# Sums of weight blocks made for two tiles by one instruction, in gate and up of a SwiGLU layer

## The chip, the cores and the metric

The kernel runs on one core of a Trainium2 chip. The metric is the device time of one execution in microseconds (us), the median of several runs. Besides TensorE (PE in the profile, PEld for its weight loads) there are VectorE (DVE), ScalarE (ACT), GpSimd (POOL) and SyncE (SP), whose queue starts most transfers.

## What is computed

One layer of a hybrid decoder: a mixing part (sliding-window attention beside an RWKV-7 recurrence, merged by gates), then a SwiGLU feed-forward part, both with RMS norms and residuals, all in float32. The change lies in the feed-forward part alone:

```python
D_MODEL, SEQ, FFN_HIDDEN = 2048, 512, 5632
h = rms_norm(x, norm_ffn[l])
x = x + (jax.nn.silu(h @ ffn_gate[l]) * (h @ ffn_up[l])) @ ffn_down[l]
return rms_norm(x, norm_final)
```

## The kernel before

**Gate and up.** The two products of 512 tokens with 2048 x 5632 weights are made in 11 chunks of 512 hidden columns (`CHUNKS`, index `j`). In a chunk the weights of 2048 rows stand in two row blocks (of gate and up each), with which a scheme of Strassen's kind works: the 2 x 2 blocks 11, 12, 21 and 22 (`wblock`, each 1024 rows by 512 columns, laid out as 4 runs of 8 tiles of 128) are combined by additions, and seven products (`PRODUCTS`, made in the order 1, 7, 6, 5, 4, 3, 2) take the place of eight. The activations have their own combinations (`S_raw`, split in `S_hi` and `S_lo`), made once, the later ones in chunk 0.

**Items.** Each product has 8 items, one for each 128-row tile `k` of its weight block (`HK` is 8); a chunk has 56, the kernel 616. An item goes through three engines. ScalarE rounds the tile to a high part (`ring_high`, tile `ring_hi`, the cast of line 697). VectorE subtracts that from the tile for the low part (`ring_low`, line 1540, tile `ring_lo`). TensorE makes six matmuls from both (lines 2150 to 2154): three for each of two groups of 128 tokens. The high and low parts lie in a ring of 4 slots (`RING`), so a cast of item w waits until item w - 4 has been multiplied (`item_done`). In products 1, 3 and 2 the tile is a block as it was loaded; in 7, 6, 5 and 4 it is a combination, and the cast waits for `sums_ready` to reach `sum_of(j, product, k)`.

**The sums.** VectorE makes them in place in the blocks: `t_one` (block 11 becomes 12 - 11, used by product 5, and by `t_two`), `t_three` (block 12 becomes 22 - 12, product 7), `t_two` (block 12 becomes 22 - 11, product 6) and `t_four` (block 12 becomes 12 - 21, product 4). One instruction makes one tile of 128 rows: 128 partitions of 4 x 128 columns, 512 in all. Each counts `sums_ready` up by one. `block_wait` holds a sum until the half block (4 tiles) has been loaded.

**Order.** VectorE's queue is written out by hand, in the loops of lines 1609 to 1697: for each product of a chunk, eight times a low part and between them the sums that later products need, and the additions that join the products: `hidden1` and `hidden2` (the products of gate and up, scaled), and additions to `u2buf`, `u3buf` and `c22buf` out of PSUM. `hidden1(j - 1)` of the chunk before stands in product 1, after low parts 5 and 6. `fence()` is a drain, an instruction that lets all earlier work of VectorE finish. TensorE makes product 1, then waits for `hidden1` and turns its result by eight transposes (line 2163), then makes product 7. In chunk 0 VectorE also makes the low parts of four activation combinations (`s_late_low`, line 1588, 2048 columns each).

Of the kernel before, what the change touches and what calls it, by code (L numbers as in the profile page):

```python
# [29 lines left out]
P = 128  # L30
# [46 lines left out]
HK = KD // 2  # L77
# [51 lines left out]

def sum_of(j, product, k):  # L130

    first = {5: k + 1 + max(k - 5, 0), 7: (2 * k + 7 if k < 3 else k + 9), 6: 2 * HK + k + 1,
             4: 3 * HK + k + 1}[product]
    return j * 4 * HK + first


PARTS = ("u2", "u3", "c22", "c21", "hid2", "c12", "hid1")
# [34 lines left out]
def build_layer(nc, xT, w_slots, w_ups, w_gu, w_down, norms, pair_cst, low_mu,  # L172
# [108 lines left out]
    def place(at, name, shape, dt=f32):  # L281

        return Arena(nc, keep.at - H_BYTES - W_BYTES + at * 1024)(name, shape, dt)
# [9 lines left out]
    wblock = {b: place(block_at[b], f"wblock{b}", [CT, HK * P]) for b in block_at}  # L293
# [23 lines left out]
    with ExitStack() as ctx:  # L317
# [91 lines left out]
        def block_wait(engine, j, b, k):  # L409

            engine.wait_ge(block_loaded[b][2 * k // HK], rows_before[b] + 16 * (j + 1))
# [683 lines left out]
        def _(dve):  # L1095
# [4 lines left out]
            def fence():  # L1100

                V.drain()  # L1102
# [433 lines left out]
            def ring_low(j, product, k):  # L1536

                w = item_of(j, product, k)
                dve.wait_ge(ring_hi_ready, w + 1)
                V.tensor_tensor(ring_lo[w % RING][:], wsrc[product][:, :, k * P:(k + 1) * P],  # L1540
                                ring_hi[w % RING][:].bitcast(f32), SUB).then_inc(ring_lo_ready, 1)
# [19 lines left out]

            def of_tile(b, k):

                return wblock[b][:, :, k * P:(k + 1) * P]

            def t_one(j, k):

                block_wait(dve, j, 12, k)
                V.tensor_tensor(of_tile(11, k), of_tile(12, k), of_tile(11, k), SUB).then_inc(sums_ready, 1)
# [10 lines left out]
            def t_four(j, k):  # L1580

                block_wait(dve, j, 21, k)
                V.tensor_tensor(of_tile(12, k), of_tile(12, k), of_tile(21, k), SUB).then_inc(sums_ready, 1)
# [25 lines left out]
            for j in range(CHUNKS):  # L1609
                last = j == CHUNKS - 1  # L1610
                for k in range(HK):
                    if j or k >= 4:
                        ring_low(j, 1, k)
                    t_one(j, k)
                    if k >= 5:
                        fence()
                        t_three(j, k - 5)
                    if j and k in (5, 6):
                        hidden1(j - 1, k - 5)
                for k in range(HK):  # L1620
                    ring_low(j, 7, k)
                    if k + 3 < HK:
                        t_three(j, k + 3)
                    else:
                        fence()
                        t_two(j, k - 5)
                    if j == 0 and k == 3:
                        dve.wait_ge(ss_done, 2)
                        V.tensor_scalar(rstd, R[2][:, 0:4], 1.0 / D_MODEL, NORM_EPS, MUL, ADD
                                        ).then_inc(ms_ready, 1)  # L1630
                    if j == 0 and k == 7:
                        dve.wait_ge(rms_ready, 2)
                        V.reciprocal(rstd, rstd)
                        fence()
                        s_late_low(0, 5)
                for k in range(HK):
                    ring_low(j, 6, k)
                    if k + 3 < HK:
                        t_two(j, k + 3)
                    if j == 0 and k == 4:  # L1640
                        s_late_low(1, 4)
                    if j == 0 and k == 7:
                        s_late_low(2, 3)
                for k in range(HK):
                    ring_low(j, 5, k)
                    if k < 3:
                        fence()
                        t_four(j, k)
                    if j == 0 and k == 2:
                        s_late_low(3, 2)  # L1650
                    if k in (3, 4):
                        dve.wait_ge(item_done, after(j, 6))
                        dve.wait_ge(c_read, copied(j, "p1", k - 3))
                        V.tensor_tensor(u2buf[:, k - 3, :], u2buf[:, k - 3, :], bank_b[k - 3][:], ADD
                                        ).then_inc(c_ready, 1)
                    if k in (5, 6):
                        fence()
                        if j:
                            dve.wait_ge(hid2_stored, 16 * j)
                        else:  # L1660
                            for u in range(2):
                                dve.wait_ge(x2_stored[u], 16 * (KD // 2 + 1))
                        V.tensor_tensor(u3buf[:, k - 5, :], u2buf[:, k - 5, :], bank_of(j, 7)[k - 5][:], ADD
                                        ).then_inc(c_ready, 1)
                for k in range(HK):
                    ring_low(j, 4, k)
                    if k + 3 < HK:
                        t_four(j, k + 3)
                    if k in (3, 4):
                        dve.wait_ge(item_done, after(j, 5))  # L1670
                        if j:
                            dve.wait_ge(hid1_stored, 16 * j)
                        fence()
                        V.tensor_tensor(c22buf[:, k - 3, :], u3buf[:, k - 3, :], bank_d[k - 3][:], ADD
                                        ).then_inc(c_ready, 1)
                for k in range(HK):
                    ring_low(j, 3, k)
                    if k in (3, 4):
                        dve.wait_ge(item_done, after(j, 4))
                        fence()  # L1680
                        V.tensor_tensor(u3buf[:, k - 3, :], u3buf[:, k - 3, :], bank_b[k - 3][:], SUB
                                        ).then_inc(c_ready, 1)
                    if k == 7:
                        hidden2(j, 0)
                    if last and k >= 5:
                        g_low(0, k - 5)
                for k in range(HK):
                    ring_low(j, 2, k)
                    if k == 0:
                        hidden2(j, 1)  # L1690
                    if k in (3, 4):
                        dve.wait_ge(item_done, after(j, 3))
                        fence()
                        V.tensor_tensor(u2buf[:, k - 3, :], u2buf[:, k - 3, :], bank_d[k - 3][:], ADD
                                        ).then_inc(c_ready, 1)
                    if last:
                        g_low(0, k + 3)
# [679 lines left out]
```

## Time and profile before

| | us |
|---|---|
| median of 3 runs | 2839.48 |
| lowest and highest | 2838.54, 2843.10 |
| the profiled execution | 2841.24 |
| its span | 2839.3 |
| gate and up in it, about | 1450 to 2330 |

The page of a profile gives busy time by engine and the costliest groups of instructions. Other views are asked of the trace: the busy time of each engine in a stretch (windows), who waited for whom (waits), and the instructions in order of time (timeline). In a timeline row stand the start, the duration, engine, line, operation, written tile and read tiles, shapes and a count, and in brackets the idle time of the engine before it and who ended that. Matmuls are shown with durations that overlap; the distance of their starts is the pace. Numbers of buffers are left out of names. The bank of PSUM that a product uses is called dense or work.

### The profile page before, as it was taken

Reading aid. Unit: us, or ns where it says so; the run is one execution under the profiler, and the core shown is the slowest. Engines: PE = TensorE matmul, PEld = TensorE weight load, DVE = VectorE, ACT = ScalarE, POOL = GpSimd, SP = SyncE. Lnnn points to the kernel's source line nnn. Section 1 sums busy time; section 2 is a strip of 40 time slices with the busy share of each in tenths; the row PEclk is TensorE's granted clock in tenths of the full one; section 3 lists DMA queues with packets and bytes.
Section 4 is the critical chain, followed back from the end, with each engine's and each line's share of the span. In section 5 each row is a group of like instructions: output and inputs, shape, how many; then the busy total and the mean of one; then the engine's idle time right before and its main releaser. Section 6 shows DMA issues by size and latency. Waiting matters only on the chain.

```text
span 2839.3 us, 37234 instructions
## 1 busy us (share of the span) xinstructions
PE 2779.1 (98%) x14475; PEld 2247.7 (79%) x14475; DVE 1532.7 (54%) x2529; ACT 1120.0 (39%) x1761; POOL 794.1 (28%) x675
## 2 busy tenths in 40 slices
PE   8999999999999999999999999999999998999998
PEld 7767777777777777888877888888888876888887
DVE  5656355365365364322478888888888861111122
ACT  5444333343333343222345555555555542222222
POOL 2333333234234234545410000000000014545454
PEclk9999999999999999999999999999999999999999
DMA  5222222222222233434344443333334434333323
GB/s 185 75 75 102 81 77 94 71 78 92 74 82 92 74 115 127 155 126 155 135 154 134 126 134 108 120 107 113 122 107 134 134 118 161 133 102 133 102 92 110
DMA packets 116862, 320.08 MB, mean 113 GB/s; under 512 B 7264, under 2 KB 23904, under 8 KB 103776
## 3 DMA queue, kind: packets, MB, share of 16 engines
q1 hardware_dynamic: 108736, 303.24, 31.7%
q10 hardware_dynamic: 7968, 14.68, 1.5%
q8 instruction: 105, 1.72, 0.2%
q14 instruction: 53, 0.43, 0.0%
HBM read 285.66 MB, written 32.24 MB: 112 GB/s over the span
## 4 chain that ended last, share of the span: by engine, by line
PE 90%; DVE 4%; ACT 2%; DMA 2%; issue 1%; DVEq 1%; POOL 0%; SPq 0%; ACTq 0%; POOLq 0%
PE dense L1773 17%; PE dense L1775 16%; PE dense L1774 16%; PE work L2150 7%; PE work L2152 7%; PE work L2154 7%; PE dense L2150 2%; PE dense L2154 2%; PE dense L2152 2%; PE work L1941 1%; PE work L1993 1%; DVEq L1102 1%; PE work L1774 1%; PE work L1773 1%; PE work L1775 1%
## 5 line engine op out<-in xcount | busy, mean ns | idle before, releaser
L655 POOL TENSOR_TENSOR wlo<-raw,whi 128x512 fp32r<-128x512 f32 x400 | 540.7, 1382 | 890.6 <-ACT whi L697 890.6
L655 POOL TENSOR_TENSOR dn_lo<-dn_raw,dn_hi 128x352 fp32r<-128x352 f32 x256 | 240.5, 971 | 1137.0 <-ACT dn_hi L697 1137.0
L697 ACT ACTIVATE ring_hi<-wblock 128x512 fp32r<-128x512 f32 x616 | 388.4, 632 | 405.2 <-PE work L2154 293.0
L1773 PE MATMUL dense<-H_hi,whi 128*128 128x512 f32 x1208 | 504.9, 418 | 10.0 <-DVE H_lo L1130 8.5
L1540 DVE TENSOR_TENSOR ring_lo<-wblock,ring_hi 128x512 fp32r<-128x512 f32 x616 | 422.0, 687 | 126.5 <-ACT ring_hi L697 120.2
L1775 PE MATMUL dense<-H_hi,wlo 128*128 128x512 f32 x1208 | 473.5, 392 | 0.0
L1774 PE MATMUL dense<-H_lo,whi 128*128 128x512 f32 x1208 | 473.2, 392 | 0.0
L2150 PE MATMUL work<-ring_hi,S_hi 128*128 128x512 f32 x976 | 383.7, 393 | 14.3 <-DVE ring_lo L1540 14.3
L697 ACT ACTIVATE whi<-raw 128x2048 fp32r<-128x2048 f32 (+1 forms) x109 | 198.2, 1821 | 470.2 <-PE dense L1775 396.2
L2152 PE MATMUL work<-ring_hi,S_lo 128*128 128x512 f32 x976 | 381.4, 391 | 0.0
L2154 PE MATMUL work<-ring_lo,S_hi 128*128 128x512 f32 x976 | 381.2, 391 | 0.0
L1773 PEld LDWEIGHTS dense<-H_hi,whi 128*128 128x128 f32 x1208 | 227.6, 188 | 81.6 <-issue 27.0
L1773 PE MATMUL dense<-G_hi,dn_hi 128*128 128x512 f32 x693 | 270.7, 391 | 10.3 <-POOL dn_lo L655 10.3
L1774 PE MATMUL dense<-G_lo,dn_hi 128*128 128x512 f32 x693 | 270.2, 390 | 0.0
L1775 PE MATMUL dense<-G_hi,dn_lo 128*128 128x512 f32 x693 | 270.1, 390 | 0.0
L1775 PEld LDWEIGHTS dense<-H_hi,wlo 128*128 128x128 f32 x1208 | 227.3, 188 | 50.0
L1774 PEld LDWEIGHTS dense<-H_lo,whi 128*128 128x128 f32 x1208 | 228.0, 189 | 45.0 <-issue 5.8
L1710 DVE TENSOR_TENSOR resid<-resid,dense 128x512 f32<-128x512 f32 x63 | 43.3, 687 | 386.5 <-PE dense L1775 386.5
L697 ACT ACTIVATE dn_hi<-dn_raw 128x1408 fp32r<-128x1408 f32 x64 | 88.4, 1382 | 359.5 <-PE dense L1775 340.0
L2150 PEld LDWEIGHTS work<-ring_hi,S_hi 128*128 128x128 f32 x976 | 184.2, 189 | 56.8 <-DVE ring_lo L1540 19.0
L2154 PEld LDWEIGHTS work<-ring_lo,S_hi 128*128 128x128 f32 x976 | 184.1, 189 | 38.8
L2152 PEld LDWEIGHTS work<-ring_hi,S_lo 128*128 128x128 f32 x976 | 184.3, 189 | 37.4
(338 smaller groups left out, 3896.4 us busy)
## 6 DMA issues: line engine op xcount, KB each, us to landing
raw<-w_slots SPq DMA_DIRECT2D x101, 1024.0 KB, 4.9
wblock<-w_gu SPq DMA_DIRECT2D x88, 1024.0 KB, 8.7
dn_raw<-w_down SPq DMA_DIRECT2D x64, 704.0 KB, 4.1
G_raw<-hidden_dram SPq DMA_DIRECT2D x4, 2816.0 KB, 11.4
gates_dram<-gout ACTq DMA_DIRECT2D x32, 256.0 KB, 2.1
gin<-gates_dram SPq DMA_DIRECT2D x16, 512.0 KB, 3.6
hidden_dram<-u3buf SPq DMA_DIRECT2D x11, 512.0 KB, 3.1
hidden_dram<-c22buf SPq DMA_DIRECT2D x11, 512.0 KB, 2.9
```

What stands on the lines that cost most here:

```text
L655: done = nc.gpsimd.tensor_tensor(rest[s][:, at], full[s][:, at], high[s][:, at].bitcast(f32), SUB)
L697: return A.activation(dst, src, ACT.Copy, scale=scale)
L1102: V.drain()
L1540: V.tensor_tensor(ring_lo[w % RING][:], wsrc[product][:, :, k * P:(k + 1) * P], ring_hi[w % RING][:].bitcast(f32), SUB).then_inc(ring_lo_r ...
L1710: V.tensor_tensor(resid[:, m, :], resid[:, m, :], dense[s][:], ADD).then_inc(bank_read, 1)
L1773: PE.matmul(bank[:], high[s][:, wk], hi[:, k, :], start=(k == first), stop=False)
L1774: PE.matmul(bank[:], high[s][:, wk], lo[:, k, :], start=False, stop=False)
L1775: done = PE.matmul(bank[:], rest[s][:, wk], hi[:, k, :], start=False, stop=(k == last))
L1941: done = PE.matmul(g_bank(2 * t + e)[:, half:half + 2 * P], src[heads[e], tok], zq[heads[e], t].rearrange("p a n -> p (a n)"), start=True, ...
L2150: PE.matmul(banks[a][:], S_hi[product][:, k, tok], high[:], start=(k == 0 and product not in (3, 2)), stop=False, skip_group_check=True)
L2152: PE.matmul(banks[a][:], S_lo[product][:, k, tok], high[:], start=False, stop=False, skip_group_check=True)
L2154: done = PE.matmul(banks[a][:], S_hi[product][:, k, tok], rest[:], start=False, stop=(k == HK - 1), skip_group_check=True)
```

## The change

A sum is made for two tiles by one instruction: 128 partitions of 4 x 256 columns, 1024 in all. `of_tile` covers two tiles, the four kinds of sum are called for even `k` only, and a chunk has 16 of them where it had 32. They are called after the odd low part of a pair. `sum_of` counts pairs. In product 1 there is now a drain ahead of each `t_one`; `t_three` for tiles 0 to 3 stands after low parts 5 and 7 of product 1, `t_two` for 0 to 3 after low parts 5 and 7 of product 7, and `t_four` for 0 to 3 after low parts 1 and 3 of product 5. Drains ahead of sums are ten a chunk; there were nine. Nothing else is changed: casts, low parts, matmuls, additions and transfers are the same and in the same order.

```diff
@@ -129,9 +129,9 @@
 
 def sum_of(j, product, k):
 
-    first = {5: k + 1 + max(k - 5, 0), 7: (2 * k + 7 if k < 3 else k + 9), 6: 2 * HK + k + 1,
-             4: 3 * HK + k + 1}[product]
-    return j * 4 * HK + first
+    pair = k // 2
+    place = {5: (1, 2, 3, 5), 7: (4, 6, 7, 8), 6: (9, 10, 11, 12), 4: (13, 14, 15, 16)}[product][pair]
+    return j * 2 * HK + place
 
 
 PARTS = ("u2", "u3", "c22", "c21", "hid2", "c12", "hid1")
@@ -1561,7 +1561,7 @@
 
             def of_tile(b, k):
 
-                return wblock[b][:, :, k * P:(k + 1) * P]
+                return wblock[b][:, :, k * P:(k + 2) * P]
 
             def t_one(j, k):
 
@@ -1611,17 +1611,19 @@
                 for k in range(HK):
                     if j or k >= 4:
                         ring_low(j, 1, k)
-                    t_one(j, k)
-                    if k >= 5:
+                    if k % 2:
+                        fence()
+                        t_one(j, k - 1)
+                    if k in (5, 7):
                         fence()
                         t_three(j, k - 5)
                     if j and k in (5, 6):
                         hidden1(j - 1, k - 5)
                 for k in range(HK):
                     ring_low(j, 7, k)
-                    if k + 3 < HK:
+                    if k in (1, 3):
                         t_three(j, k + 3)
-                    else:
+                    elif k in (5, 7):
                         fence()
                         t_two(j, k - 5)
                     if j == 0 and k == 3:
@@ -1635,7 +1637,7 @@
                         s_late_low(0, 5)
                 for k in range(HK):
                     ring_low(j, 6, k)
-                    if k + 3 < HK:
+                    if k in (1, 3):
                         t_two(j, k + 3)
                     if j == 0 and k == 4:
                         s_late_low(1, 4)
@@ -1643,9 +1645,9 @@
                         s_late_low(2, 3)
                 for k in range(HK):
                     ring_low(j, 5, k)
-                    if k < 3:
+                    if k in (1, 3):
                         fence()
-                        t_four(j, k)
+                        t_four(j, k - 1)
                     if j == 0 and k == 2:
                         s_late_low(3, 2)
                     if k in (3, 4):
@@ -1664,7 +1666,7 @@
                                         ).then_inc(c_ready, 1)
                 for k in range(HK):
                     ring_low(j, 4, k)
-                    if k + 3 < HK:
+                    if k in (1, 3):
                         t_four(j, k + 3)
                     if k in (3, 4):
                         dve.wait_ge(item_done, after(j, 5))
```

## Rows read from the trace of the kernel before

**Rows 1.** the page: busy time by engine, costliest group on VectorE

```profile
PE 2779.1 (98%) x14475; PEld 2247.7 (79%) x14475; DVE 1532.7 (54%) x2529; ACT 1120.0 (39%) x1761; POOL 794.1 (28%) x675
...
L1540 DVE TENSOR_TENSOR ring_lo<-wblock,ring_hi 128x512 fp32r<-128x512 f32 x616 | 422.0, 687 | 126.5 <-ACT ring_hi L697 120.2
```

**Rows 2.** stretches: length, busy PE, PEld, DVE, ACT, POOL, PEclk, DMA, GB/s

```profile
1450.00:1530.00 80.00, 71.17 (x306) 57.19 (x305) 70.34 (x107) 43.53 (x67) 0.00 (x0) 0.98 0.45 143
1850.00:1930.00 80.00, 79.99 (x362) 66.07 (x361) 67.10 (x105) 41.36 (x67) 0.00 (x0) 1.00 0.41 126
```

**Rows 3.** waits, 1530 to 2290 us: who <- whom, us, times, longest

```profile
DVE ring_lo L1540 <- ACT ring_hi L697: 100.4, 146, 1.6
...
ACT ring_hi L697 <- DVE wblock L1574: 33.0, 30, 2.0
...
PEld work L2150 <- DVE ring_lo L1540: 2.2, 5, 0.4
...
PEld dense L2150 <- DVE ring_lo L1540: 2.2, 5, 0.4
```

**Rows 4.** VectorE timeline, chunk 5: start us, us, line, tile, [idle]

```profile
1856.71 0.69 DVE L1540 TENSOR_TENSOR ring_lo<-wblock,ring_hi 128x512 fp32r<-128x512 f32 x1
1857.32 0.68 DVE L1569 TENSOR_TENSOR wblock<-wblock,wblock 128x512 f32<-128x512 f32 x1
1858.09 0.69 DVE L1574 TENSOR_TENSOR wblock<-wblock,wblock 128x512 f32<-128x512 f32 x1
1858.70 0.74 DVE L1594 SCALAR_TENSOR_TENSOR u2buf<-u2buf,rstd,c22buf 128x512 f32<-128x512 f32 x1
1859.37 0.68 DVE L1540 TENSOR_TENSOR ring_lo<-wblock,ring_hi 128x512 fp32r<-128x512 f32 x1
...
1862.02 0.68 DVE L1540 TENSOR_TENSOR ring_lo<-wblock,ring_hi 128x512 fp32r<-128x512 f32 x1
...
1864.00 0.68 DVE L1540 TENSOR_TENSOR ring_lo<-wblock,ring_hi 128x512 fp32r<-128x512 f32 x1
```

**Rows 5.** ScalarE timeline, same stretch: the cast of item (1, 5)

```profile
1856.04 0.63 ACT L697 ACTIVATE ring_hi<-wblock 128x512 fp32r<-128x512 f32 x1 [0.15 <-PE dense L2154]
```

**Rows 6.** TensorE timeline, same stretch: first matmuls of items, and the transposes

```profile
1861.22 0.39 PE L2150 MATMUL dense<-ring_hi,S_hi 128*128 128x512 f32 x1
...
1862.75 0.50 PE L2150 MATMUL dense<-ring_hi,S_hi 128*128 128x512 f32 x1
...
1864.24 1.04 PE L2163 MATMUL work<-cst,u2buf 128*128 128x128 f32 x8
...
1865.04 0.47 PE L2150 MATMUL work<-ring_hi,S_hi 128*128 128x512 f32 x1
...
1866.51 0.39 PE L2150 MATMUL work<-ring_hi,S_hi 128*128 128x512 f32 x1
```

**Rows 7.** VectorE timeline, 1024 and 2048 columns and what follows each

```profile
286.63 1.23 DVE L1395 TENSOR_TENSOR Y<-a_in,block_of 128x1024 f32<-128x1024 f32 x1
287.77 0.68 DVE L1155 TENSOR_TENSOR gout<-rstd,dense 128x512 f32<-128x512 f32 x1
...
1486.25 2.28 DVE L1588 TENSOR_TENSOR S_lo<-S_raw,S_hi 128x2048 fp32r<-128x2048 f32 x1
1488.45 1.89 DVE L1540 TENSOR_TENSOR ring_lo<-wblock,ring_hi 128x512 fp32r<-128x512 f32 x3
```

**Rows 8.** TensorE timeline, chunk 0: first matmuls of items that came late

```profile
1460.85 0.80 PE L2150 MATMUL work<-ring_hi,S_hi 128*128 128x512 f32 x1 [4.47 <-DVE ring_lo L1540]
...
1480.96 0.50 PE L2150 MATMUL work<-ring_hi,S_hi 128*128 128x512 f32 x1 [1.01 <-DVE ring_lo L1540]
...
1489.19 0.50 PE L2150 MATMUL work<-ring_hi,S_hi 128*128 128x512 f32 x1 [1.13 <-DVE ring_lo L1540]
...
1499.56 0.50 PE L2150 MATMUL work<-ring_hi,S_hi 128*128 128x512 f32 x1 [1.82 <-DVE ring_lo L1540]
...
1501.05 0.40 PE L2150 MATMUL work<-ring_hi,S_hi 128*128 128x512 f32 x1
```

## Prediction

> **What bounds the kernel now.** I read the page first: TensorE is busy for 98% of the span and VectorE for 54% [rows 1], but these are means over stages, so the next view is the busy time by stretch, and there VectorE works 67.10 of 80 us in a steady chunk of gate and up while TensorE works 79.99 of them [rows 2]. Both are nearly full; TensorE sets the pace. The waits say the same: over chunks 1 to 10 the low parts (ring_lo) wait 100.4 us for the casts of ScalarE, so VectorE has slack, and TensorE waits for a low part only ten times, once a chunk, 0.4 us each [rows 3]. The one place per chunk where VectorE is late is found in the timelines. I write (p, k) for item k of product p. An item starts every 1.36 us on TensorE; (1, 6) starts at 1861.22, so (1, 7) was due at 1862.58 and started at 1862.75, because its low part began at 1862.02 on VectorE [rows 4, 6]. So a low part's start plus 0.73 us is the earliest start of its item, and the item that was waited for takes 0.13 us more (1864.24 less 1862.75 is 1.49). In products 1 and 7 VectorE is given more than 1.36 us of work an item: that corner decides what the edit does. Chunk 0 is different: there TensorE is busy for only 71.17 of 80 us [rows 2] and stands four times for a low part, 4.47, 1.01, 1.13 and 1.82 us [rows 8].
>
> **What an instruction costs.** From start to start, not by its duration: two neighbours of 512 columns lie 0.60 us apart (1857.32 less 1856.71 is 0.61) though each is shown with 0.68. A drain between them makes it 0.77, so a drain is 0.17 us; the product of hidden1 takes 0.67 (1859.37 less 1858.70) [rows 4]. The edit's instruction has 1024 columns. The only one of that width is an addition elsewhere, 1.14 us from start to start, and 2048 columns take 2.20 [rows 7]; the straight line from 0.60 to 2.20 gives 1.13 for 1024. I take 1.14. Bounds: 1.07 below, which is 512 columns at that line's slope (1.60 us for 1536, so 0.533) twice with no fixed part at all, and 1.23 above, the duration shown for the addition, as if nothing overlapped. So a wide sum saves 2 x 0.60 - 1.14 = 0.06 us, sixteen a chunk save 1.0 us, and against it stands one drain more (ten for nine). That is a gain of 0.8 us of VectorE's time a chunk, 9 us in eleven chunks, none of it on TensorE's path as such.
>
> The Trainium skill's page "VectorE: DVE Perf Modes", section "The TRN2 errata — SBUF-src ops pay a fixed extra latency per instruction", has (N+151)/0.96 ns for an fp32 tensor_tensor and advises large tiles; an estimate by it gives 157 ns saved for each pair, 2.5 us a chunk. The spacing in the trace speaks for the Trainium skill's other figure, some 75 ns an instruction after overlap ("Vector Engine (DVE) Microarchitecture Reference", section "Measured stream behaviour on trn2"). The sum goes by the spacing.
>
> **Where the work moves, steady chunk.** This is the part that counts. In product 1 the queue of VectorE held between low part (1, 5) and low part (7, 0): 3 of t_one, 3 of t_three, 2 of hidden1, the low parts (1, 5), (1, 6) and (1, 7), and 3 drains. That is 9 x 0.60 + 2 x 0.67 + 3 x 0.17 = 7.25, and the rows have 1864.00 - 1856.71 = 7.29 [rows 4], so the method holds. After the edit: t_one for tiles 4 and 5, t_three for 0 and 1, t_one for 6 and 7, t_three for 2 and 3. These are eight tiles where six were, in four wide instructions, with four drains: 3 x 0.60 + 4 x 1.14 + 2 x 0.67 + 4 x 0.17 = 8.38. (The fourth tile of t_three was made in product 7 and the fifth of t_one before (1, 5).)
>
> Is VectorE early enough at (1, 5)? Its cast starts at 1856.04 when TensorE frees the ring slot, and the low part follows at 1856.71, 0.67 us later [rows 4, 5]. I walk from low part (1, 2), which now stands behind the first wide t_one: cast starts are 1.36 apart, so (1, 1) can start at 1851.27; drain and wide sum bring (1, 2) to 1853.18, (1, 3) is again bound by its cast at 1853.99, then drain and wide sum bring (1, 4) to 1855.90, and (1, 5) could go at 1856.50 but waits for its cast until 1856.71. So it starts as before, with 0.21 us in hand, and the early drains cost nothing.
>
> From there: (1, 6) starts at 1856.71 + 0.60 + 0.17 + 1.14 + 0.17 + 1.14 + 0.67 = 1860.60 and is ready at 1861.33 for an item due at 1861.22: 0.11 us late, 0.24 with the slow first item. (1, 7) starts 0.60 + 0.67 later at 1861.87, ready at 1862.60, while TensorE reaches it at 1861.33 + 1.49 = 1862.82: the stall of today goes. Then (7, 0) starts at 1856.71 + 8.38 = 1865.09 and is ready at 1865.82. TensorE ends (1, 7) at 1864.18, does the eight transposes (0.80 us, 1864.24 to 1865.04 [rows 6]) and stands from 1864.98 to 1865.82. The next item starts at 1865.82 + 1.49 = 1867.31, where it was 1866.51 [rows 6]: 0.80 us lost a chunk. hidden1 is done at about 1861.9, before the transposes ask for it.
>
> What is queued behind: the casts of (7, 2) and (7, 3) need t_three 2 and 3, done at about 1865.2 and used from 1867.4, covered. In product 7 VectorE then has four wide sums and two drains for 8 items, 8 x 0.60 + 4 x 1.14 + 2 x 0.17 = 9.7 us against 10.9 of TensorE, and its low parts stay ahead: (7, 2) ready 1868.16 for 1868.67, (7, 6) ready 1873.0 for 1874.1. In product 5 the item k = 3 holds a low part, a drain, a wide t_four and an addition, 2.51 us for 1.36, so it falls back 1.15 us; a low part that starts on its cast is 2.4 us ahead of its item (cast at 1856.04, low part ready at 1857.44, item (1, 5) due at 1859.86), so this is covered, and would cost nothing until VectorE fell back by twice as much. SP's loads wait for low parts of product 5 and later, whose pace is TensorE's. The pairs 0-1, 2-3 and 4-5, 6-7 lie within the halves in which a block is loaded, so no sum waits for a transfer that it didn't need. All this moves 0.8 us in each of ten chunks: +8.0 us.
>
> **Chunk 0.** Here VectorE's queue is the path, and what it has done before each of TensorE's stands counts. Before (1, 4) it makes 4 tiles of t_one: two wide and two drains, 2 x 1.31 = 2.62 for 2.41, 0.2 us later; later stands absorb that. Before (6, 0): 20 tiles in 10 wide where 19 were, two drains more, and 0.34 us of waiting for a block that falls away: 0.60 - 0.64 + 0.34 - 0.34, no change, so (6, 0) starts at 1480.9. Before (6, 5) five narrow t_two become two wide: 0.7 us earlier. Before (5, 3) one wide t_four and one drain replace three of each: 1.0 us earlier still, 1.7 in all. But the second wide t_four then stands before (5, 4), which is ready only 0.4 us earlier than before; TensorE had 0.3 us in hand there (low part (5, 3) starts 0.73 before 1499.56, then 0.60 and an addition of 0.60, then 0.73 again: ready 1500.76 for 1501.05 [rows 8]), so it gains 0.7 and after the slow item 0.6. Taken: -0.6 us, with -1.7 and +0.4 as bounds.
>
> **Sum.** 8.0 - 0.6 = +7.4 us. The profiled execution took 2841.24 us, 2839.3 of it the span; it would become 2848.6. It lies 1.8 us above the median of 2839.48, which becomes 2846.9, 0.26% more. Differences under 0.2%, 5.7 us, can hardly be told from none in a measurement of this kernel. Bounds of the steady term: with 1.07 a wide sum the loss falls by 4 x 0.07 to 0.52 a chunk, with 1.23 it rises by 0.36 to 1.16; so 5 to 12 us, and 3.5 to 12 with chunk 0.
>
> **Rivals.** First, the corner is covered after all: the queue between (1, 5) and (7, 0) would have to be 0.84 us shorter than my sum. Then TensorE never stands there, today's 0.30 us at (1, 7) goes in ten chunks and chunk 0 gives its full 1.7: -4.7 us, 2834.8. It decides when a wide sum with its drain costs 0.2 us less than 1.31. Both lower bounds together, 1.07 and drains that hide behind a wide sum for two of the four, give only 0.6: (7, 0) is then 0.24 us late and ends 0.2 later than today, +2.0 in ten chunks, and with chunk 0 the time is 2840 to 2841. The spacing of [rows 7] speaks against it. Chance of a gain above 0.2% by this way 0.07, of the half way 0.2.
>
> Second, fewer instructions free VectorE and the time follows its busy share: 2.4 us a chunk by durations (32 x 0.68 less 16 x 1.23), 26 us in all, 2813. Against it: TensorE is busy 79.99 of 80 us [rows 2], so there is nothing to win outside chunk 0. Chance 0.01.
>
> Third, the wide form is slow where it reads and writes four runs of 256 columns in place, say 2 x 0.68 = 1.37 each. Then (7, 0) comes 4 x 0.23 = 0.9 us later still, 1.7 us a chunk, +17 us, 2856. The narrow sums in four runs of 128 keep the 0.60 of contiguous ones, which speaks against it. Chance 0.07.
>
> Fourth, the edit doesn't do what it says, the sums being hidden wherever they are: TensorE's pace is unchanged, 2839.5. It needs the low part (7, 0) to be ready by 1865.04. Chance 0.05.
>
> **Chances.** My forecast, a loss of 3.5 to 12 us, has 0.60, of which some 0.15 lies under 5.7 us. So slower 0.52, same 0.40, faster 0.08. The range 2840 to 2853 takes in the bounds of the sum and the half-covered case.
>
> **What would show it.** In the changed kernel's waits TensorE should wait once a chunk for a low part, before the first item of product 7, 0.8 to 1.0 us, in place of 0.4 before (1, 7), and a trace of 0.1 at (1, 6). The sums should appear 176 times at 1.22 us, and 1.14 from start to start. From low part (1, 5) to low part (7, 0) should be 8.4 us where it is 7.29. In chunk 0 the stand before (5, 3) should shrink from 1.82 to about 1.1 and a new one of 1.0 appear before (5, 4). A spacing under 1.05, or no stand at (7, 0), would make the prediction wrong.

## The result and the profile after

The changed kernel is slower: the ratio of its time to that of the kernel before is 1.0034 (95% interval 1.0021 to 1.0047), medians of 2851.58 and 2840.66 us in five runs each. Timed again beside later experiments it was 1.0029 (1.0017 to 1.0041), 2851.53 against 2841.94. The ratio is not that of the medians: by the ratios the changed kernel loses 9.7 and 8.2 us, by the medians 10.9 and 9.6.

The page after the change, busy time by engine and the group that stands in [rows 1]:

```profile
PE 2783.0 (98%) x14475; PEld 2248.3 (79%) x14475; DVE 1521.2 (53%) x2353; ACT 1118.4 (39%) x1761; POOL 794.8 (28%) x675
...
L1540 DVE TENSOR_TENSOR ring_lo<-wblock,ring_hi 128x512 fp32r<-128x512 f32 x616 | 416.5, 688 | 145.7 <-ACT ring_hi L697 142.2
```

VectorE works 11.5 us less in the whole (1532.7 to 1521.2), in 176 instructions fewer, and TensorE does the same work in a span 8.5 us longer. The stretches of [rows 2] after the change (length, busy PE, PEld, DVE, ACT, POOL, granted clock, DMA share, GB/s):

```profile
1450.00:1530.00 80.00, 71.43 (x303) 56.54 (x302) 69.35 (x91) 43.57 (x67) 0.00 (x0) 0.98 0.45 144
1850.00:1930.00 80.00, 79.32 (x357) 65.37 (x357) 65.14 (x87) 41.21 (x67) 0.00 (x0) 1.00 0.39 119
```

In the steady stretch TensorE is now idle for 0.68 of 80 us, where it was 0.01. The waits say where. Waits over the same ten chunks as [rows 3] (who waited for whom: us in total, times, longest):

```profile
DVE ring_lo L1540 <- ACT ring_hi L697: 120.1, 188, 1.6
...
PEld dense L2152 <- issue: 4.5, 5, 0.9
PEld work L2152 <- issue: 4.4, 5, 0.9
PE work L2152 <- DVE ring_lo L1540: 3.7, 6, 0.7
PE dense L2152 <- DVE ring_lo L1540: 3.5, 5, 0.7
PEld work L2152 <- DVE ring_lo L1540: 2.3, 5, 0.7
PEld dense L2152 <- DVE ring_lo L1540: 2.0, 5, 0.4
```

Where TensorE waited ten times, it now waits twice a chunk for a low part: up to 0.4 us ahead of a weight load, before item (1, 6), and about 0.7 us ahead of a matmul, before (7, 0). The 0.9 us that the profile puts under "issue" of a weight load are the same stand before (7, 0), seen from the weight load. VectorE itself waits more for casts than it did, 120.1 us for 100.4, so it has more time over in the whole, and yet it is late in one place. That place is in the timeline. VectorE in chunk 5, the stretch that answers to [rows 4]:

```profile
1859.60 1.49 DVE L1540 TENSOR_TENSOR ring_lo<-wblock,ring_hi 128x512 fp32r<-128x512 f32 x2
1861.17 1.23 DVE L1569 TENSOR_TENSOR wblock<-wblock,wblock 128x1024 f32<-128x1024 f32 x1
1862.49 1.23 DVE L1574 TENSOR_TENSOR wblock<-wblock,wblock 128x1024 f32<-128x1024 f32 x1
1863.63 0.75 DVE L1594 SCALAR_TENSOR_TENSOR u2buf<-u2buf,rstd,c22buf 128x512 f32<-128x512 f32 x1
1864.30 0.69 DVE L1540 TENSOR_TENSOR ring_lo<-wblock,ring_hi 128x512 fp32r<-128x512 f32 x1
1864.90 0.74 DVE L1594 SCALAR_TENSOR_TENSOR u2buf<-u2buf,rstd,c22buf 128x512 f32<-128x512 f32 x1
1865.56 0.69 DVE L1540 TENSOR_TENSOR ring_lo<-wblock,ring_hi 128x512 fp32r<-128x512 f32 x1
1866.34 1.23 DVE L1569 TENSOR_TENSOR wblock<-wblock,wblock 128x1024 f32<-128x1024 f32 x1
1867.65 1.23 DVE L1574 TENSOR_TENSOR wblock<-wblock,wblock 128x1024 f32<-128x1024 f32 x1
1868.80 1.28 DVE L1540 TENSOR_TENSOR ring_lo<-wblock,ring_hi 128x512 fp32r<-128x512 f32 x2
```

The first row holds low parts (1, 4) and (1, 5); (1, 5) starts at 1859.60 + 1.49 - 0.69 = 1860.40. Low part (7, 0) is the first of the last row: 8.40 us after it, where [rows 4] have 7.29. The wide sums of the stretch (1861.17, 1862.49, 1866.34, 1867.65) last 1.23 us, and the next thing starts 1.14 us after one, or 1.31 with a drain. TensorE, first matmuls of items (1, 6), (1, 7), the transposes, (7, 0) and (7, 1), as in [rows 6]:

```profile
1865.04 0.50 PE L2152 MATMUL dense<-ring_hi,S_hi 128*128 128x512 f32 x1
...
1866.53 0.40 PE L2152 MATMUL dense<-ring_hi,S_hi 128*128 128x512 f32 x1
...
1867.92 1.03 PE L2165 MATMUL work<-cst,u2buf 128*128 128x128 f32 x8
1869.63 0.47 PE L2152 MATMUL work<-ring_hi,S_hi 128*128 128x512 f32 x1 [0.68 <-DVE ring_lo L1540]
...
1871.09 0.40 PE L2152 MATMUL work<-ring_hi,S_hi 128*128 128x512 f32 x1
```

The transposes start at 1867.92 and take 0.80 us, so (7, 0) could start at 1868.72; it starts at 1869.63, 0.91 us later. Before the change it followed the transposes at once.

### The profile page after: what moved, and what is told of

The parts are those of the page before. It is cut to its first block, busy times and chain, and to the rows that moved or that the text cites. A ratio compares the mean times of both kernels' runs of the same rounds, so it can differ in the third digit from the quotient of the medians.

```text
span 2847.8 us, 37069 instructions
## 1 busy us (share of the span) xinstructions
PE 2783.0 (98%) x14475; PEld 2248.3 (79%) x14475; DVE 1521.2 (53%) x2353; ACT 1118.4 (39%) x1761; POOL 794.8 (28%) x675
## 3 DMA queue, kind: packets, MB, share of 16 engines
q8 instruction: 105, 1.72, 0.2%
## 4 chain that ended last, share of the span: by engine, by line
PE 88%; DVE 6%; ACT 2%; DMA 1%; issue 1%; DVEq 1%; POOL 0%; ACTq 0%; SPq 0%; POOLq 0%
PE dense L1775 17%; PE dense L1777 16%; PE dense L1776 16%; PE work L2152 7%; PE work L2156 7%; PE work L2154 7%; PE dense L2152 2%; PE dense L2156 1%; PE dense L2154 1%; DVE ring_lo L1540 1%; PE work L1943 1%; DVE wblock L1569 1%; DVE wblock L1574 1%; DVEq L1102 1%; PE work L1995 1%
```

## Experiments

Every kernel here is compared with the kernel before in runs on the same chip. Beside the time I give the period of a steady chunk: from the transposes of hidden1 in chunk 1 to those in chunk 10, divided by nine. In the kernel before that is (2255.54 - 1551.24) / 9 = 78.26 us, in the changed one (2263.70 - 1550.95) / 9 = 79.19, and again 79.19 in the first run below. The period comes from one execution and leaves out the early stages and chunk 0. In some executions it contains one stand of VectorE of 0.35 us for which the trace shows no cause ("issue"); where it falls in the corner, as in chunk 4 of the changed kernel in both of its traces, it adds 0.04 to the period, so differences of that size mean nothing. The last column is worked out from rows and good to 0.01 us.

| kernel | ratio (95% interval) | period, us | (1, 5) to (7, 0) on VectorE, us |
|---|---|---|---|
| before | 1 | 78.26 | 7.29 |
| changed, again (r1) | 1.0029 (1.0017 to 1.0041) | 79.19 | 8.40 |
| t_three later (r2) | 1.0012 (1.0003 to 1.0021) | 78.76 | 7.08 |
| t_three and t_four later (r3) | 1.0015 (1.0006 to 1.0024) | 78.77 | 7.09 |
| narrow, same places (r4) | 1.0045 (1.0032 to 1.0059) | 79.44 | 8.67 |
| narrow, hidden1 later (r5) | 0.9990 (0.9981 to 0.9999) | 78.04 | 7.30 |
| wide, spread (r6) | 0.9996 (0.9987 to 1.0005) | 78.14 | 7.09 |
| narrow, spread (r7) | 1.0020 (1.0011 to 1.0029) | 78.75 | 7.30 |
| t_one alone wide (r8) | 1.0025 (1.0016 to 1.0034) | 78.89 | 8.13 |
| t_three alone wide (r9) | 1.0000 (0.9991 to 1.0009) | 78.37 | 7.57 |
| r5, t_two and t_four wide (r10) | 0.9995 (0.9986 to 1.0004) | 78.10 | 7.29 |
| change in chunk 0 alone (r11) | 1.0001 (0.9992 to 1.0010) | 78.27 | 7.29 |

**r1, the changed kernel again.**

> The changed kernel itself, timed on the same chip as the next three. Earlier it took 1.0034 of the kernel before. Theory (the corner: two tiles of sums too many stand on VectorE between low part (1, 5) and low part (7, 0), so TensorE stands before item (7, 0) in each of ten chunks): 9 to 11 us over before, with one stand of about 0.7 us a chunk. Rival (chance of the chip or of the run): nearer to before.

Measured: 9.6 us over before by the medians, 8.2 by the ratio, with the period of the first profile. The loss is not one chip's.

**r2, one wide sum moved out of the corner.**

```diff
-                    if k in (5, 7):
+                    if k == 5:
                         fence()
                         t_three(j, k - 5)
...
                     ring_low(j, 7, k)
+                    if k == 0:
+                        fence()
+                        t_three(j, 2)
                     if k in (1, 3):
                         t_three(j, k + 3)
```

> The changed kernel, with the wide t_three for tiles 2 and 3 moved from behind low part (1, 7) to behind low part (7, 0), its drain with it; all else wide as in the change. Theory of the corner: low part (7, 0) starts 1.31 us earlier, 7.1 us after (1, 5) where it was 8.4, the stand before (7, 0) is gone in all ten chunks, a stand of 0.1 to 0.2 at (1, 6) stays in place of the one at (1, 7) of the kernel before: some 9 to 10 us faster than the changed kernel, 0 to 2 us faster than before. Rival (wide sums or ten drains cost VectorE time wherever they stand): within 2 us of the changed kernel, 8 to 11 us over before.

The stand before (7, 0) is gone and (7, 0) comes 7.08 us after (1, 5), as expected; the time falls from 1.0029 to 1.0012. But it should have fallen to before or under it, and 0.50 us a chunk stay. VectorE and TensorE in chunk 5 of this kernel, low parts (7, 0), (7, 1), the sum for tiles 4 and 5, low parts (7, 2) and (7, 3), then the first matmul of item (7, 2):

```profile
1869.50 0.69 DVE L1540 TENSOR_TENSOR ring_lo<-wblock,ring_hi 128x512 fp32r<-128x512 f32 x1
...
1871.42 0.68 DVE L1540 TENSOR_TENSOR ring_lo<-wblock,ring_hi 128x512 fp32r<-128x512 f32 x1
1872.02 1.22 DVE L1574 TENSOR_TENSOR wblock<-wblock,wblock 128x1024 f32<-128x1024 f32 x1
1873.16 1.28 DVE L1540 TENSOR_TENSOR ring_lo<-wblock,ring_hi 128x512 fp32r<-128x512 f32 x2
```

```profile
1873.90 0.49 PE L2155 MATMUL work<-ring_hi,S_hi 128*128 128x512 f32 x1
```

Low part (7, 1) at 1871.42 is ready at 1872.15 for an item due at 1872.18, and (7, 2) at 1873.16 is ready at 1873.89 for an item due at 1873.54: the stand has moved two items on. It is 0.36 us long and the item takes 0.13 more, which is the 0.50. The theory had gone no further than (7, 0). Both theories stated beforehand miss the number; which of them holds is told by r4 to r9.

**r3, the second wide t_four of product 5 moved as well.**

```diff
-                    if k in (1, 3):
+                    if k in (1, 7):
                         fence()
-                        t_four(j, k - 1)
+                        t_four(j, 0 if k == 1 else 2)
```

> As the run before this one, and the wide t_four for tiles 2 and 3 moved from behind low part (5, 3) to behind (5, 7). Theory: in chunk 0 the stand before (5, 4) goes, 0.7 to 1.0 us less than the run before this one, and nothing changes in the other ten chunks, where product 5 has 2.4 us in hand; 1 to 3 us faster than before. Rival (VectorE is as late in product 5 of every chunk): 7 us less than the run before this one.

The period is that of r2 (78.77 for 78.76), so product 5 of a steady chunk has time in hand, as the prediction had it. The 0.7 to 1.0 us in chunk 0 can't be seen in the time: the ratios of r2 and r3 lie within each other's intervals. The traces show them: the stand before (5, 4) is gone in r3, and from the start of item (6, 0) to the transposes of chunk 1 it takes 68.99 us (1481.84 to 1550.83) where r2 takes 70.02 (1484.68 to 1554.70). That r3 would be faster than before by 1 to 3 us was a miss, for the same rest as in r2.

**r4, places without width.** The changed kernel with each wide sum written as two narrow ones.

```diff
-                return wblock[b][:, :, k * P:(k + 2) * P]
+                return wblock[b][:, :, k * P:(k + 1) * P]
...
-                V.tensor_tensor(of_tile(11, k), of_tile(12, k), of_tile(11, k), SUB).then_inc(sums_ready, 1)
+                V.tensor_tensor(of_tile(11, k), of_tile(12, k), of_tile(11, k), SUB)
+                V.tensor_tensor(of_tile(11, k + 1), of_tile(12, k + 1), of_tile(11, k + 1), SUB).then_inc(sums_ready, 1)
```

and so for the other three kinds.

> The changed kernel's places, drains and semaphore counts, but each wide sum made by two narrow ones of 512 columns: place without width. Theory (place is what costs, width gives 0.06 us a pair): low part (7, 0) comes 8.6 us after (1, 5), 0.25 us later than in the changed kernel, 2.5 us in ten chunks and about 0.6 in chunk 0: 12 to 14 us over before. Rival (the wide form itself is slow, or VectorE's queue is blocked longer by it): back to before, within 2 us.

12.8 us over before, inside the 12 to 14 expected. VectorE, low parts (1, 4) with (1, 5), and (7, 0) with (7, 1):

```profile
1861.57 1.42 DVE L1540 TENSOR_TENSOR ring_lo<-wblock,ring_hi 128x512 fp32r<-128x512 f32 x2
...
1870.97 1.28 DVE L1540 TENSOR_TENSOR ring_lo<-wblock,ring_hi 128x512 fp32r<-128x512 f32 x2
```

(1, 5) starts at 1861.57 + 1.42 - 0.69 = 1862.30 and (7, 0) 8.67 us later, 0.27 more than with wide sums, and the period is 0.25 longer. Four pairs stand between them, so a pair made wide saves 0.06 to 0.07 us. The wide form is not what costs; the place is.

**r5, nothing wide, the corner relieved.**

```diff
                     if j or k >= 4:
                         ring_low(j, 1, k)
+                    if j and k in (6, 7):
+                        hidden1(j - 1, k - 6)
                     t_one(j, k)
...
-                    if j and k in (5, 6):
-                        hidden1(j - 1, k - 5)
```

> The kernel before (all sums narrow), with the two instructions of hidden1 moved from behind low parts (1, 5) and (1, 6) to directly behind (1, 6) and (1, 7). Nothing is wide. Theory (the corner is all there is to win in a steady chunk): low part (1, 7) starts 0.67 us earlier, the stand before item (1, 7) goes, (7, 0) is just in time: 0.30 us less in each of ten chunks, 3 us, a ratio of about 0.9990. Rival (hidden1 is now late for the transposes): a stand before them instead, no gain.

0.9990, 2.3 us less than before (2839.04 against 2841.38). No wait of TensorE for a low part is listed over chunks 1 to 10, and the period is 0.22 shorter. 0.30 was expected; (7, 0) still starts 0.1 us after the transposes end. By its ratio and its period this is the fastest kernel here, though the times don't tell it from r6 and r10 below, and it has no wide sum.

**r6 and r7, a better order, wide and narrow.** In r6 the wide sums are spread, and hidden1 stands as in r5:

```diff
-                    if k % 2:
+                    if j and k in (6, 7):
+                        hidden1(j - 1, k - 6)
+                    if k in (1, 3, 5):
                         fence()
                         t_one(j, k - 1)
...
                     ring_low(j, 7, k)
-                    if k in (1, 3):
-                        t_three(j, k + 3)
-                    elif k in (5, 7):
+                    if k == 1:
+                        t_three(j, 4)
+                    if k == 3:
+                        fence()
+                        t_one(j, 6)
+                    if k == 4:
+                        fence()
+                        t_three(j, 6)
+                    if k == 6:
                         fence()
-                        t_two(j, k - 5)
+                        t_two(j, 0)
...
                     ring_low(j, 6, k)
+                    if k == 0:
+                        fence()
+                        t_two(j, 2)
```

with t_four as in r3. r7 is r6 with each wide sum written as two narrow ones, as in r4.

> All sums wide as in the change, but spread so that no more than one or two wide ones stand between two low parts: hidden1 as in the run before this one; t_three for 2, 3 behind (1, 7), for 4, 5 behind (7, 1); t_one for 6, 7 behind (7, 3), t_three for 6, 7 behind (7, 4); t_two for 0, 1 behind (7, 6), for 2, 3 behind (6, 0); t_four for 2, 3 behind (5, 7). Theory: walking VectorE's queue with 0.60, 0.67, 1.14 and 0.17 us, every low part of a steady chunk is in time by 0.1 us or more: 3 us less than before in ten chunks, and chunk 0 gains up to 1.5 more: ratio 0.998 to 0.999. Rival (wide sums cost TensorE something beyond the queue of VectorE, or the second run's rest of 0.4 us a chunk has another cause than low parts (7, 1) and (7, 2)): a stretch of ten chunks 4 us longer than before, as in that run.

> The places and drains of the run before this one, each wide sum made by two narrow ones. Theory (width gives 0.06 us a pair of VectorE's time, and where VectorE is in time that is worth nothing): within 1.5 us of it, the steady chunks alike. Rival (the gain of that kernel comes from its width): 3 us or more slower than it.

r6 has a period of 78.14, and the late low parts (7, 1) and (7, 2) that made the rest of r2 are gone: that rest was late low parts. Its time is not told from before, 0.9996. The theory of r6, every low part in time by 0.1 us or more and 3 us gained in ten chunks, missed: low part (6, 2) is late. Low part (6, 2), first in its row, and the first matmuls of items (6, 1), (6, 2) and (6, 3) in r6:

```profile
1879.14 1.29 DVE L1540 TENSOR_TENSOR ring_lo<-wblock,ring_hi 128x512 fp32r<-128x512 f32 x2
```

```profile
1878.48 0.39 PE L2161 MATMUL work<-ring_hi,S_hi 128*128 128x512 f32 x1
...
1879.88 0.50 PE L2161 MATMUL work<-ring_hi,S_hi 128*128 128x512 f32 x1
...
1881.38 0.39 PE L2161 MATMUL work<-ring_hi,S_hi 128*128 128x512 f32 x1
```

(6, 2) was due at 1878.48 + 1.36 = 1879.84, its low part is ready at 1879.87, and the item takes 1.50 us. So r6 gains 0.30 in the corner and gives back 0.18 here, which makes its 0.12 a chunk.

r7 was expected within 1.5 us of r6 and is 6.6 us slower (2846.82 against 2840.23), 0.61 a chunk. Low part (6, 2), first in its row, and the first matmul of item (6, 2) in r7:

```profile
1884.11 1.28 DVE L1540 TENSOR_TENSOR ring_lo<-wblock,ring_hi 128x512 fp32r<-128x512 f32 x2
```

```profile
1884.85 0.50 PE L2165 MATMUL work<-ring_hi,S_hi 128*128 128x512 f32 x1 [0.15 <-DVE ring_lo L1540]
```

From low part (1, 5) to low part (6, 2) VectorE takes 21.02 us in r6 (1858.12 to 1879.14) and 21.65 in r7 (1862.46 to 1884.11). Nine pairs lie between, so a pair made wide saves 0.07 us there. The 0.61 is lost in three places: 0.10 before (7, 0), some 0.2 in the items from (7, 6) to (6, 0), after item (7, 5) had to wait for its low part, and 0.3 at (6, 2), which starts 1.72 us after (6, 1) where r6 has 1.40. So the rival of r7 holds: in an order in which VectorE waits for only 0.2 us in these thirteen items, the width of the sums adds up and is worth 0.6 us a chunk. The distance from (1, 5) to (7, 0) alone would not have told it: it is 7.30 in r7 as it is in r5.

**r8 and r9, one kind of sum wide at a time.** The kernel before, with t_one (r8) or t_three (r9) made wide at the change's places:

```diff
-                    t_one(j, k)
+                    if k % 2:
+                        fence()
+                        t_one(j, k - 1)
```

```diff
-                    if k >= 5:
+                    if k in (5, 7):
                         fence()
                         t_three(j, k - 5)
...
-                        t_three(j, k + 3)
+                        if k in (1, 3):
+                            t_three(j, k + 3)
```

> The kernel before with t_one alone made wide, at the change's places and with its drain; t_three, t_two and t_four narrow and where they were. Theory: between low parts (1, 5) and (7, 0) stand 3 low parts, 2 wide, 3 narrow sums, 2 of hidden1 and 5 drains, 8.07 us: (1, 7) is 0.25 late and (7, 0) 0.4, 0.5 us a chunk, 5 us over before. Rival (the whole loss comes from the pairs of t_three): within 1.5 us of before.

> The kernel before with t_three alone made wide, at the change's places (for 0, 1 behind low part (1, 5), for 2, 3 behind (1, 7), the rest behind (7, 1) and (7, 3)); t_one, t_two and t_four narrow and where they were. Theory: one tile more than before in the corner but a drain less, 7.56 us from low part (1, 5) to (7, 0); the stand before (1, 7) goes and one of 0.3 to 0.4 before (7, 0) comes: between 0 and 0.1 us a chunk, within 1.5 us of before. Rival (the pairs of t_three carry the loss): 0.5 us or more a chunk.

t_one alone costs 1.0025, 0.63 us a chunk (0.5 expected). t_three alone costs nothing that the time shows (1.0000); its period is 0.11 longer, of which 0.04 is one stand of VectorE without a shown cause, in chunk 8. Low parts (1, 4) with (1, 5), and (7, 0), in r8:

```profile
1863.13 1.48 DVE L1556 TENSOR_TENSOR ring_lo<-wblock,ring_hi 128x512 fp32r<-128x512 f32 x2
...
1872.05 0.69 DVE L1556 TENSOR_TENSOR ring_lo<-wblock,ring_hi 128x512 fp32r<-128x512 f32 x1
```

From 1863.13 + 1.48 - 0.69 = 1863.92 to 1872.05 are 8.13 us. Put in a row with the table: 8.13, 8.40 and 8.67 us give periods 0.63, 0.93 and 1.18 over before. Each 0.27 us more in the corner costs 0.25 to 0.30 us a chunk, once (7, 0) is what TensorE waits for. Both r8 and r9 have seven tiles of sums in the corner, but r8 has five drains there and r9 two, since a pair of t_one brings a drain and a pair of t_three saves one: 3 x 0.17 of the 0.56 us between 8.13 and 7.57.

**r10, wide only where it is cheap.** r5 with t_two and t_four wide, t_two for tiles 0 and 1 behind (7, 5), for 2 and 3 behind (6, 0), t_four for 2 and 3 behind (5, 7).

```diff
-                    else:
+                    elif k == 5:
                         fence()
-                        t_two(j, k - 5)
+                        t_two(j, 0)
...
-                    if k < 3:
+                    if k in (1, 7):
                         fence()
-                        t_four(j, k)
+                        t_four(j, 0 if k == 1 else 2)
```

> The kernel of the fifth run (narrow sums, hidden1 later), with t_two and t_four alone made wide: t_two for 0, 1 behind low part (7, 5), for 2, 3 behind (6, 0), t_four for 2, 3 behind (5, 7), the rest behind the odd low parts. The corner stays as in the fifth run. Theory: steady chunks as in the fifth run, 0.2 to 0.3 us a chunk under before; in chunk 0, where VectorE's queue is the path, four drains fewer and 0.06 us a pair: up to 1.4 us less. Ratio to before 0.998 to 0.999. Rival (pairs cost wherever they are): over the fifth run by 2 us or more.

0.9995 against 0.9990 of r5, each beside the kernel before on its own chip, and a period of 78.10 against 78.04: the pairs cost nothing there and bring nothing that can be measured. The 1.4 us less in chunk 0 are not seen.

**r11, the change in chunk 0 alone.**

```diff
-                    t_one(j, k)
+                    if j:
+                        t_one(j, k)
+                    elif k % 2:
+                        fence()
+                        t_one(j, k - 1)
```

and so for the other three kinds.

> The change in chunk 0 alone; chunks 1 to 10 have the narrow sums and places of the kernel before. Prediction's term for chunk 0: -0.6 us, bounds -1.7 and +0.4. What the trace of the changed kernel suggests: 0.5 us more than before, because VectorE, ahead by then, waits 0.57 us for a cast that stands behind the cast of an activation block, and is held 0.4 us longer before an addition in product 5. Rival (chunk 0 carries a good part of the 9 us): 3 us or more over before.

1.0001 (0.9992 to 1.0010): chunk 0 carries none of the loss that can be seen in the time, and no gain above 2.3 us. The time doesn't tell a term of -0.6 from one of +0.5 us. The trace does lean to the second: from item (1, 2) to the transposes of chunk 1 r11 takes 98.29 us (1452.48 to 1550.77), the changed kernel 98.32 and the kernel before 97.87.

## Why the prediction was right, and where it was off

**The corner.** The step that carried the forecast held to a few hundredths of a microsecond: from low part (1, 5) to (7, 0) 8.40 us for 8.38 worked out, a wide sum with 1.14 from start to start and a drain with 0.17, TensorE late by 0.1 at (1, 6), not at (1, 7), and standing after the transposes. r8, the changed kernel and r4 lengthen that distance step by step, and the period follows; r5 removes the stand at (1, 7) without any wide sum and gains. That is shown. At 7.6 us and under the distance alone does not tell the period: r5 and r7 have 7.30, and r5 gains 0.22 a chunk where r7 loses 0.49; r2 has 7.08 and loses 0.50. There low parts further on are late, and a walk that ends at (7, 0), as in the theory of r2, misses them. The prediction's walk went on through product 7, and there its low parts stayed ahead as it said: (7, 2) is ready at 1871.87 for an item that starts at 1872.47.

**Its size.** The term was 0.80 us a chunk and measured 79.19 - 78.26 = 0.93. The step that fell short is "a low part's start plus 0.73 us is the earliest start of its item". At (1, 6) it held (1864.30 to 1865.04), at (7, 0), behind the transposes, it took 0.83 (1868.80 to 1869.63), 0.10 more. Of the rest, 0.02 is the distance from (1, 5) to (7, 0), (7, 0) itself took 1.46 us for the 1.49 of my sum and (7, 1) 1.38 for 1.36. That makes 0.91, and the one stand of 0.35 us in chunk 4 puts 0.04 on the period. In ten chunks it is 9.3 us for 8.0.

**Chunk 0.** Predicted -0.6, and here the sign was wrong as far as the traces tell. In them, from the late start of item (1, 2) to the transposes of chunk 1, the kernel before takes 97.87 us (1453.37 to 1551.24) and the changed one 98.32 (1452.63 to 1550.95), and again 99.36 in r1. The stands of the changed kernel that answer to the last ones of [rows 8]:

```profile
1480.93 0.50 PE L2152 MATMUL work<-ring_hi,S_hi 128*128 128x512 f32 x1 [1.41 <-DVE ring_lo L1540]
...
1488.41 0.50 PE L2152 MATMUL work<-ring_hi,S_hi 128*128 128x512 f32 x1 [0.39 <-DVE ring_lo L1540]
...
1497.75 0.50 PE L2152 MATMUL work<-ring_hi,S_hi 128*128 128x512 f32 x1 [0.85 <-DVE ring_lo L1540]
...
1500.26 0.50 PE L2152 MATMUL work<-ring_hi,S_hi 128*128 128x512 f32 x1 [0.86 <-DVE ring_lo L1540]
```

These are the stands before (6, 0), (6, 5), (5, 3) and (5, 4). The one before (5, 3) shrank from 1.82 to 0.85, where 1.1 was expected to be left, and the new one before (5, 4) is there, 0.86 for 1.0. But the one before (6, 0) grew from 1.01 to 1.41: from (1, 2) to (6, 0) it is 28.30 us (1452.63 to 1480.93) for 27.59 (1453.37 to 1480.96), 0.71 more, where the sum had no change. My count took VectorE's queue for the only path. VectorE and ScalarE between (7, 6) and (7, 7):

```profile
1474.56 0.68 DVE L1540 TENSOR_TENSOR ring_lo<-wblock,ring_hi 128x512 fp32r<-128x512 f32 x1
1475.81 0.69 DVE L1540 TENSOR_TENSOR ring_lo<-wblock,ring_hi 128x512 fp32r<-128x512 f32 x1 [0.57 <-ACT ring_hi L697]
```

```profile
1473.36 1.90 ACT L697 ACTIVATE S_hi<-S_raw 128x2048 fp32r<-128x2048 f32 x1
1475.16 1.13 ACT L697 ACTIVATE ring_hi<-wblock 128x512 fp32r<-128x512 f32 x2
```

Low part (7, 7) waited 0.57 us for its cast, and that stood on ScalarE behind the cast of an activation block (S_hi, 1.90 us). VectorE was early there and could not use it: the next thing to be late was ScalarE's order. From (6, 0) to the transposes of chunk 1 the changed kernel then gained 0.26 us (70.28 to 70.02) for the 0.6 of the sum. Items (5, 6) and (5, 7) were late too, 1.52 and 1.51 us for 1.36; the sum had ended its walk at (5, 4). r11 has the same two stretches, 28.30 and 69.99.

The 99.36 of r1 has another cause, and the trace shows it. VectorE waited there for a block of weights, ahead of t_three for tiles 0 and 1:

```profile
1464.51 1.23 DVE L1574 TENSOR_TENSOR wblock<-wblock,wblock 128x1024 f32<-128x1024 f32 x1 [1.34 <-DMA wblock<-w_gu]
```

VectorE was idle for 1.34 us, item (1, 6) then stood for 0.55 us, and from (1, 2) to (6, 0) r1 takes 29.32 us for 28.30. r2 and r3 have the same wait, 1.25 and 1.30 us, the kernel before one of 0.34. So a single trace gives the term of chunk 0 within about 1 us: near +0.45 where the load is in time.

**The sum.** 9.3 for the steady chunks and about 0.45 for chunk 0 make 9.7, against 7.4 predicted and 8.2 to 10.9 measured. The predicted median of 2846.9 was 4.7 us under the measured 2851.58. Of these 1.2 are in the median of before, which rose from 2839.48 in three runs to 2840.66 in five, 1.3 in the steady term and 1.0 in chunk 0; for the last 1.2 no trace has a place, and the runs of one kernel spread by more than that. The chances were wide on the slow side: the part of my forecast that lay under 5.7 us rested on bounds of the wide sum's spacing, 1.07 to 1.23, while the row of the one instruction of that width had given 1.14 and the runs have 1.14.

**The rivals.** The covered corner did not happen. That fewer instructions free VectorE and the time follows is refuted as it was put (11.5 us less busy time, 9 us more in all); r6 against r7 shows where it is true. Its price had a slip that changes nothing: 32 x 0.68 less 16 x 1.23 is 2.1 us a chunk and not 2.4, which gives 2817 and not 2813. The slow wide form is refuted by r4. That the change does nothing is refuted by the result.

The fixed cost of an instruction, 75 ns by the Trainium skill ("Vector Engine (DVE) Microarchitecture Reference", section "Measured stream behaviour on trn2"), is what r4 and r7 show, 0.06 to 0.07 us a pair. An estimate by the 151 cycles of the Trainium skill's "VectorE: DVE Perf Modes", section "The TRN2 errata — SBUF-src ops pay a fixed extra latency per instruction", would give 0.16 for a pair, and the runs disagree with that for work that is queued back to back.

## What to carry to other kernels

When an engine that feeds another runs close to its pace, don't judge a batched instruction by the time it saves but walk the feeder's queue through the tightest stretch, item by item, until it has caught up again, and not only to the first item that is late: what is pulled into the stretch counts fully (here 8.40 us for 7.29, two more tiles and a drain), the saved fixed cost only by 0.06 to 0.07 us a pair. That small saving adds up where the queue is full for many items (0.6 us a chunk in r6 against r7) and is worth nothing where it is not (r10). Then move work that has no early user, here hidden1, behind what the bound engine waits for; that alone (0.9990) gave as much as any order with wide sums. Price instructions from start to start.

## What was not expected of the hardware

In chunk 0 TensorE stands for 4.5 to 4.8 us before (1, 4). After it its matmuls of 512 columns, else 0.23 us apart, are 0.43 apart for a while; in the kernel before the granted clock is 0.50 from 1461.0 to 1463.0, which is the lower of its two levels, 1.2 GHz for 2.4. That lasted for 6 matmuls in r5, 7 in the kernel before ([rows 8] show its first, with 0.80), 8 in the changed one and 13 in r2, r8 and r10, though TensorE's work was the same. It does not explain the 1 us between the two traces of the changed kernel, in which it lasted for 8 matmuls each; the late load does.

A shorter stand can bring it too. In r5 and r8 the clock fell again after the stands of 1.82 and 1.86 us before (5, 3), and seven or eight matmuls ran 0.43 apart. r8, the first three matmuls of (5, 3), and the stretch from 1503 to 1506 us (length, busy PE, PEld, DVE, ACT, POOL, granted clock, DMA share, GB/s):

```profile
1502.66 0.71 PE L2168 MATMUL work<-ring_hi,S_hi 128*128 128x512 f32 x1 [1.86 <-DVE ring_lo L1556]
1503.17 0.63 PE L2170 MATMUL work<-ring_hi,S_lo 128*128 128x512 f32 x1
1503.60 0.63 PE L2172 MATMUL work<-ring_lo,S_hi 128*128 128x512 f32 x1
```

```profile
1503.00:1506.00 3.00, 3.00 (x8) 2.32 (x8) 2.84 (x6) 0.40 (x1) 0.00 (x0) 0.50 0.00 0
```

That costs 1.6 us in r5 and r8: from the start of (5, 3) to that of (5, 5) they take 4.45 us, the kernel before 2.87 and r9 2.88. The last two stood there for 1.82 and 1.84 us and kept the clock at 1.00, so the length of the stand alone does not decide it, and what does stays open. The stands in the corner of chunks 1 to 10, up to 0.8 us, never brought it; what they cost beyond themselves is 0.13 us in the item behind (1.49 for 1.36), and the item after that took 1.39 us for 1.36.
